# Gates and ups in seven products of quarters, for the last two token blocks of a two-layer fp32 kernel

## The reference

```python
h2 = rmsnorm(x, norm2_g[l])
gate = jnp.einsum('bsd,df->bsf', h2, w_gate[l])      # 1024 -> 2816
up = jnp.einsum('bsd,df->bsf', h2, w_up[l])          # 1024 -> 2816
x = x + jnp.einsum('bsf,fd->bsd', jax.nn.silu(gate) * up, w_down[l])
return rmsnorm(x, final_norm_g)
```

## Time and profile before

| | |
|---|---|
| median of 3 runs | 3772.93 us (3771.32 to 3776.09) |
| profiled execution, its own time | 3776.57 us |
| its span in the trace | 3774.2 us |
| busy: PE, PEld | 3707.6 us (98%), 3087.4 us (82%) |
| busy: DVE, ACT, POOL | 1829.6 us (48%), 1381.0 us (37%), 462.8 us (12%) |
| DMA | 799.34 MB, mean 212 GB/s |
| stage E and F of token block 2 | 2919 to 3342 us |
| stage E and F of token block 3 | 3342 to 3774 us |

### The profile page before, as it was taken

How to read it: one execution, slowest core, us unless ns; L and a number is a source line. 1 busy time by engine, 2 the same in 40 slices (tenths; PEclk the granted TensorE clock), 3 DMA queues, 4 the chain that set the end, 5 groups by cost and what they waited for, 6 DMA issues and landing times.

```text
span 3774.2 us, 58634 instructions
## 1 busy us (share of the span) xinstructions
PE 3707.6 (98%) x24136; PEld 3087.4 (82%) x24136; DVE 1829.6 (48%) x3365; ACT 1381.0 (37%) x2503; POOL 462.8 (12%) x237
## 2 busy tenths in 40 slices
PE   8999999999999999999999999999999999999999
PEld 6888788978897888976887779888777888887887
DVE  5657625451644455557655665554654222232223
ACT  4332421321232454565656655545552200020001
POOL 2001130000000000233233330000001000000000
PEclk9999999999999999999999999999999999999999
DMA  8756686557655877866666656545325655464554
GB/s 309 273 185 229 236 290 245 209 202 251 218 193 194 279 254 245 272 208 223 228 224 219 207 197 225 169 148 180 130 104 187 229 189 190 181 236 175 184 199 158
DMA packets 198874, 799.34 MB, mean 212 GB/s; under 512 B 20816, under 2 KB 70224, under 8 KB 130384
## 3 DMA queue, kind: packets, MB, share of 16 engines
q1 hardware_dynamic: 198608, 795.59, 60.7%
HBM read 594.18 MB, written 201.33 MB: 211 GB/s over the span
## 4 chain that ended last, share of the span: by engine, by line
PE 92%; DVE 4%; ACT 2%; issue 1%; DMA 1%; SPq 0%; DVEq 0%; ACTq 0%
PE bank L1402 87%; PE bank L1406 4%; DVE P L2484 1%; DVE P L2486 1%; DVE R L2145 0%; ACT P L1940 0%; ACT P L1939 0%; DVE Z1a L2192 0%; DVE Qb L2235 0%; SPq L2688 0%; DVE Tb L2236 0%; DMA slot<-Wd 0%; ACT L1939 0%; DMA KS<-Kd 0%; DVE Kb L2237 0%
## 5 line engine op out<-in xcount | busy, mean ns | idle before, releaser
L1402 PE MATMUL bank<-Z1a,slot 128*128 128x512 f32 x3048 | 786.1, 402 | 9.4 <-DVE slot L2083 9.4
L1402 PE MATMUL bank<-Z1b,slot 128*128 128x512 f32 x3048 | 780.9, 401 | 4.5 <-DVE Z1b L2192 4.4
L1402 PE MATMUL bank<-slot,Z0b 128*128 128x512 f32 (+1 forms) x3504 | 708.9, 353 | 7.2 <-DVE AF L2214 5.3
L1402 PEld LDWEIGHTS bank<-Z1a,slot 128*128 128x128 f32 x3048 | 568.0, 190 | 141.2 <-DVE slot L2083 9.4
L1402 PEld LDWEIGHTS bank<-Z1b,slot 128*128 128x128 f32 x3048 | 565.5, 189 | 139.1 <-issue 6.8
L1402 PEld LDWEIGHTS bank<-slot,Z0b 128*128 128x128 f32 x3504 | 563.0, 189 | 99.8 <-DVE AF L2214 6.0
L2648 POOL TENSOR_TENSOR slot<-raw,slot 128x1024 fp32r<-128x1024 f32 x110 | 289.9, 2643 | 645.5 <-ACT slot L1823 645.4
L2145 DVE SCALAR_TENSOR_TENSOR R<-bank,small,R 128x512 f32<-128x512 f32 x352 | 261.1, 749 | 208.2 <-PE bank L1402 207.7
L1402 PE MATMUL bank<-KS,DQ 128*128 128x512 f32 (+3 forms) x960 | 281.4, 389 | 9.3 <-DMA KS<-Kd 4.8
L2452 DVE TENSOR_SCALAR_CACHE_REDUCE P<-bank 128x512 f32<-128x512 f32 (+3 forms) x320 | 189.2, 608 | 199.0 <-PE bank L1402 198.4
L2660 POOL TENSOR_TENSOR Z0b<-AF,Z0b 128x512 fp32r<-128x512 f32 x88 | 126.6, 1439 | 1235.2 <-ACT Z0b L2013 1235.2
(11 more groups left out here) (235 smaller groups left out, 4551.2 us busy)
## 6 DMA issues: line engine op xcount, KB each, us to landing
slot<-Wd SPq DMA_DIRECT2D x390, 1024.0 KB, 4.9
Wd<-slot SPq DMA_DIRECT2D x130, 1024.0 KB, 6.8
raw<-in_wts_dram SPq DMA_DIRECT2D x130, 512.0 KB, 4.2
DQ<-Qd SPq DMA_DIRECT2D x192, 128.0 KB, 3.7
DV<-Vd SPq DMA_DIRECT2D x60, 256.0 KB, 4.5
KS<-Kd SPq DMA_DIRECT2D x24, 512.0 KB, 7.5
KS<-Kd SPq DMA_DIRECT2D x24, 384.0 KB, 6.9
zraw<-Yd SPq DMA_DIRECT2D x16, 512.0 KB, 5.5
```

The lines of the kernel that those rows point to most:

```text
L1402: return e.matmul(o, a, b, start=start, stop=stop, skip_group_check=True)
```

## The change

For token blocks 2 and 3 and slices 1 to 10, gate and up of a block b are taken as one product of 2 x 2 quarters: rows are gate and up, the 1024 input features are cut in two halves of 512, and the tokens in two halves of 256. Winograd's form of Strassen's algorithm needs seven products of quarters instead of eight; each is 4 x 3 matmuls of 256 columns. The order is 11, ST2, ST1, ST3, S4, T4, 12. Three banks are in use by one block (rotating over five that attention used before): 11 and then 12 add into the first, ST2, ST3 and T4 into the second, ST1 and S4 into the third, and what stands in a bank is read between two products.

- Four sums of weight quarters (S1 to S4) are made for each block: the two tiles are loaded once more as given (2 x 512 KB), GpSimd makes four adds of 128 x 512 (`sa`), ScalarE the large parts (`sh`), VectorE the small parts (`sl`).
- Four sums of feature quarters are made once per token block (`ta` on GpSimd, 128 x 1024 each, `th`, `tl`). For them, ScalarE writes each transposed feature group a second time, unsplit (`Bt`).
- ScalarE copies product 11 (`p1`); VectorE adds it or a former sum to each product (`cx`, 5 adds of 128 x 256), and the gate's factors are multiplied in two halves.
- Of the up's tile only the second half is loaded from `Wd`.
- Gates, ups and their two evictions at these blocks are gone: 2 x 24 matmuls of 512 columns.

```diff
+SEVEN = (2, 3)
+P_11, P_ST2, P_ST1, P_ST3, P_S4, P_T4, P_12 = range(7)
+SEVEN_BANKS = (2, 3, 4, 5, 6)
+SEVEN_ROLE = (0, 1, 2, 1, 2, 1, 0)
...
-            self.evac(label, ("act", 600), ("dve", 750))
+            self.evac(label, ("act", 1250 if s in SEVEN else 600), ("dve", 750))
...
+    def weight_sums(self, s):
...
+        for b in range(2, NF):
+            t = 0.0
+            if b > 2:
+                yield ("sa", s, b - 1)
+                t = P.end["sa", s, b - 1]
+            for x in range(2):
+                t = self.dma(("rf", s, b, x), 524288, t)
+            yield t
...
+            if b > 2:
+                yield ("sl", s, b - 1, 3)
+                yield P.end["sl", s, b - 1, 3]
+            t = P.put(("sa", s, b), ("pool", 5300), after=t)
+            if b > 3:
+                yield ("pr", s, b - 2, P_S4)
...
+        for i in (1, 0, 2, 3):
+            t = P.put(("sh", s, b, i), ("act", 610), after=t)
+            yield t
+            P.put(("sl", s, b, i), ("dve", 690), after=t)
...
+            P.put(("pr", s, b, i), ("pe", 12 * 117), after=t)
+            now = P.clock["pe"] + 180
+            if i == P_11:
+                P.put(("p1", s, b), ("act", 400), after=now)
+            elif i == P_12:
+                P.put(("ev", ("Fg", s, b)), ("dve", 850), ("act", 640), after=now)
+                P.put(("ev", ("Fu", s, b)), ("dve", 700))
+            else:
+                P.put(("cx", s, b, i), ("dve", 430), after=now)
...
+            def product(s, b, i):
...
+                elif i == P_ST3:
+                    pe.wait_ge(*dve_cx("cx", s, b, P_ST2))
+                elif i == P_S4:
+                    pe.wait_ge(*dve_cx("cx", s, b, P_ST1))
+                elif i == P_T4:
+                    pe.wait_ge(*dve_cx("cx", s, b, P_ST3))
+                else:
+                    pe.wait_ge(*act_p1("p1", s, b))
...
+                for k in range(4):
...
+                    mm(o, hi[:, tok(k)], bh, k == 0 and i in (P_11, P_ST2, P_ST1), False)
+                    mm(o, hi[:, tok(k)], bl, False, False)
+                    x = mm(o, lo[:, tok(k)], bh, False, k == 3)
...
+            def partial(s, b, i):
...
+                if i == P_ST2:
+                    to, x = pu[:, :], p1[:, :]
+                elif i == P_ST1:
+                    to, x = py[:, :], p1[:, :]
...
+                e.tensor_tensor(to, o, x, ALU.add).then_inc(*dve_cx.inc("cx", s, b, i))
...
+            def seven_gate(s, b):
+                g = GS[b % 2]
+                dve.wait_ge(*dve_cx("cx", s, b, P_S4))
+                e.tensor_tensor(g[:, 256:512], g[:, 256:512], factors[:, 256:512], ALU.mult)
+                dve.wait_ge(*pe_pr("pr", s, b, P_12))
+                e.tensor_tensor(g[:, 0:256], bank[seven_bank(s, b, P_12)][:, 0:256], factors[:, 0:256], ALU.mult).then_inc(
+                    *dve_g.inc("ev", ("Fg", s, b)))
...
+            def weight_sums(s, b):
+                g, u = (x[:, :].rearrange("p (a n) -> p a n", a=2) for x in raw)
+                for i in range(2):
+                    pool.wait_ge(*d_rf[i]("rf", s, b, i))
+                if b > 2:
+                    pool.wait_ge(*dve_sh("sl", s, b - 1, 3))
...
+                sums = ((u[:, 0, :], u[:, 1, :], ALU.add), (SF[:, 0, :], g[:, 0, :], ALU.subtract),
+                        (g[:, 0, :], u[:, 0, :], ALU.subtract), (g[:, 1, :], SF[:, 1, :], ALU.subtract))
...
+            def weights_as_given(s, b, x):
+
+                if b > 2:
+                    sp.wait_ge(*pool_sa("sa", s, b - 1, 3))
```

More of the change, by code:

```diff
@@ L183, in weight_order, with tile_blocks @@
     return order
+UPS = [T_F + 4 * sl + 2 * max(0, sl - 1) + 2 * k + 1 for sl in range(NF // 2) for k in range(2)]
+def tile_blocks(S):
+    order = weight_order(S)
+    n = len(order) - S * (N_TILES - T_E)
+    return [((i - n) // (N_TILES - T_E) if i >= n else -1, t) for i, t in enumerate(order)]
 def chunks(n):
@@ L214, in __init__ @@
         self.used = {}
+        self.pairs, self.pair_tiles = [], {}
+        self.halved = {i for i, (s, t) in enumerate(tile_blocks(S)) if s in SEVEN and t in UPS[2:]}
         self.G = {}
@@ L259, in fetch @@
             else:
-                P.end[("w", j)] = self.dma(("wf", j), 1048576, t)
+                P.end[("w", j)] = self.dma(("wf", j), 524288 if j in self.halved else 1048576, t)
     def left(self, j):
-        self.P.end["left", j] = self.P.end[("mm",) + self.used[j]]
+        self.P.end["left", j] = self.P.end[self.used[j]]
         self.fetch()
@@ L323, in mm @@
         for j in tiles:
-            self.used[j] = (label, part)
+            self.used[j] = ("mm", label, part)
     def evac(self, label, *steps):
@@ L767, in phase_e @@
             P.add(self.features2(s, cg), True)
+        if s in SEVEN:
+            P.add(self.token_sums(s), True)
+            P.add(self.weight_sums(s), True)
         P.add(self.norm2(s), True)
@@ L816, in phase_f @@
                     yield ("ev", ("Fu", s, 0))
+                if s in SEVEN and sl:
+                    yield from self.seven(s, b, t)
+                    P.add(self.split_act(s, b), True)
+                    t += 2
+                    continue
                 yield from self.fm(("Fg", s, b), t, 1, zr, ("dve", 690), ("act", 610), behind=() if b else (("ev", ("rb", s)),))
@@ L826, in phase_f, with seven @@
         P.put(("F done", s))
+    def seven(self, s, b, t):
+        P = self.P
+        jg, ju = yield from self.take(2, t)
+        self.pairs.append((s, b))
+        self.pair_tiles[s, b] = (jg, ju)
+        for i in range(7):
+            t = P.end["w", ju if i == P_T4 else jg]
+            if i in (P_ST1, P_ST2, P_ST3, P_S4):
+                k = ("sl", s, b, {P_ST1: 0, P_ST2: 1, P_ST3: 2, P_S4: 3}[i])
+                yield k
+                t = max(t, P.end[k])
+            if i in (P_ST1, P_ST2, P_ST3, P_T4):
+                k = ("tl", s, {P_ST1: 0, P_ST2: 1, P_ST3: 2, P_T4: 3}[i])
+                yield k
+                t = max(t, P.end[k])
+            yield t
+            P.put(("pr", s, b, i), ("pe", 12 * 117), after=t)
[7 more added lines that the diff above has]
+                P.put(("cx", s, b, i), ("dve", 430), after=now)
+            if i == P_T4:
+                self.used[ju] = ("pr", s, b, i)
+                self.left(ju)
+            yield None
+        self.used[jg] = ("pr", s, b, P_12)
+        self.left(jg)
     def split_act(self, s, b):
@@ L1190, in build @@
         pool_as = signal("pool_ff", of("as"))
+        pool_ta = signal("pool_token_sums", of("ta"))
+        pool_sa = signal("pool_weight_sums", [st + (i,) for st in of("sa") for i in range(4)])
         pool_cv = signal("pool_conv", of("cv halo"))
@@ L1198, in build @@
         d_z = landed("d_z", of("zf"))
+        d_rf = [landed(f"d_rf{i}", [st for st in of("rf") if st[3] == i]) for i in range(2)]
         d_R = [landed(f"d_R{c}", [st for st in order if st[0] in ("x0 in", "x1 in") and st[-1] == c]) for c in range(NT)]
@@ L1253, in weights_used @@
         def weights_used(j):
-            label, part = plan.used[j]
+            st = plan.used[j]
+            if st[0] == "pr":
+                return pe_pr(*st)
+            _, label, part = st
             return pe_g("ev", label) if final(part, label) else pe_half("half", label)
@@ L2117, in group_out @@
                 if by_act(label) and label not in gates:
+                    return
+                if ph in ("Fg", "Fu") and label[1:] in plan.pairs:
+                    (seven_gate if ph == "Fg" else seven_up)(s, label[2])
                     return
```

188 lines of the change are left out of this document (185 added, 3 removed).

## The result

| | before | after |
|---|---|---|
| median (range), four runs each on one chip | 3774.51 (3771.32 to 3777.41) | 3736.72 (3732.92 to 3738.93) |
| ratio (95% interval) | | 0.9899 (0.9882 to 0.9916) |
| span of the profiled execution | 3774.2 | 3731.2 |

The profiled execution after took 3732.92 us, the lowest of its four, and had the highest mean granted clock of them (0.996, the others 0.993 to 0.995). Between the spans lie 43.0 us, between the medians 37.8. The forecast was 46 by its own sum and a median of 3727.

A forecast was written before the change was run, and what follows sets the result against it. TensorE was taken to bound the kernel. Matmuls -56.0, waits in blocks +3, stage starts +4, first changed blocks +3 gave -46 us: 3776.6 to 3730.6, as a median 3727, range 3717 to 3755.

The forecast's parts named there:

- Matmuls: Gates and ups in 40 blocks: 11.20 us removed, 9.80 added per block, a gain of 56.0 us.
- no fixed cost to be seen: 256-column matmuls, read from the projection stage: 116.7 ns each, with no fixed cost on top.
- Rival 3: Seven products: shorter matmuls run slower than in the projection; at 133 ns the gain would be gone; chance 0.03.
- Waits inside a block: TensorE waiting for VectorE's reads between products: 0.08 us per block, 3 us in all, bounds 0 and 16.
- Turns: VectorE operations with two SBUF inputs and GpSimd operations wait for each other, up to 1.29 us per weight part.
- seven us: ScalarE's 0.42 us copy of product 11 was said to have seven us before it is needed.
- Supply: Weight sums for the next block, made while earlier blocks multiply: an 11.2 us cycle, hidden in 15.4, no cost.
- 4 us to spare: Margin claimed for making weight sums: a cycle of 11.2 us within the block's 15.4.
- Start of a stage: Second ScalarE pass over transposed features at two feed-forward starts: 2.1 us each, 4 in all, bounds 1 and 9.
- I assume it stays of that length: Slow clock after the wait at a feed-forward start: twelve matmuls take 4.42 us instead of 2.96, assumed unchanged.
- First changed blocks: First changed blocks of each feed-forward stage, waiting for their sums: 3 us in all, bounds 0 and 10.
- rival 1: Weight parts wait 1.29 us on GpSimd, delaying reads: 1.3 us per block, about 3776; full 0.05, partial (3740 to 3755) 0.22.

The follow-up runs named there:

- e_all32: Changed kernel with 32 unused bytes per partition ahead of everything, slots included, and 32 more ahead of the activations; span 3719.0 us.
- e_best2: e_align with SH moved on by another 32 bytes and the plain copy of the last two transposed features made last; median 3719.42 us, ratio 0.9852.
- e_slotw: Changed kernel with four products reading the gate's tile in its slot instead of the weight sums, which are still made; span 3730.2 us.
- e_read2: Changed kernel with VectorE's adds of products from PSUM to an SBUF partial each done twice; span 3742.7 us.
- F2: Not a run: the feed-forward stage of token block 2; 375.30 us in the kernel before, 353.14 in the changed one.
- F3: Not a run: the feed-forward stage of token block 3, with the tail; 383.6 us in the kernel before, 359.0 in the changed one.
- E2: Not a run: the projection stage ahead of the feed-forward stage of token block 2; 48.11 us in the kernel before, 1.66 more in the changed one.
- E3: Not a run: the projection stage between the feed-forward stages of token blocks 2 and 3; 47.89 us in the kernel before, 49.53 in the changed one.
- e_quiet: Changed kernel without sums, second weight loads or extra feature pass; the seven products read plain features and the gate's tile; span 3725.4 us.
- e_align: Changed kernel with 32 unused bytes per partition moving activations, token sums and weight sums onto a multiple of 64; span 3718.5 us.

## Right and wrong, step by step

1. **Matmuls, the mis-sized term.** "116.7 ns each" for the new products, from the earlier trace rows, was 120.0 for 48 and 118.3 for 36 of a block's 84. 0.43 us in each of 20 rounds is 8.6 us less gain. The count (84 for 48) and the 233.3 held. The form was taken from the right row, but "no fixed cost to be seen" was read from a place where the operands lay otherwise: slot as moving and Z as stationary operand, the reverse of the products. That the 120.0 comes from SH and the operand beside it having the same remainder, e_all32 and e_best2 show, and e_slotw fits. The rest, 118.3 against 116.7, is not explained; the projection of block 2, with 117.8 for 204 matmuls, was a sign in the kernel before that 116.7 can't be counted on. Rival 3 (slower than in the projection) is true by 3 ns, a sixth of the way to the 133 at which it would have decided.
2. **Waits inside a block, right, the cost too high.** Forecast 3 us (0 to 16), measured none in the steady rounds; e_read2 shows how near it was. Turns occur and are paid by idle engines. One reading was wrong and did no harm: the copy of product 11 has not "seven us", since the read of ST2 already adds it (`partial` takes `p1`). In the round shown it ends at 3135.93 and that read starts at 3136.99, so it has 1.06 us to spare.
3. **Supply, right.** Hidden in the steady state, with less room than "4 us to spare" says: 2.6 us more per block cost 16 us in F2 and F3, most of it in the first blocks; 5.2 more cost 100. What the estimate lacked is the chain of queues behind a late sum.
4. **Start of a stage, right.** Forecast 2 x 2.1 us, 4 in all; the projections E2 and E3 lost 1.65 each (1.1 of it the longer waits on Z1a shown above), the wait on Z1b 0.73 each: 4.8. The timeline shows the row of work that was foretold, with the plain copy (L1990) between the split passes:

```profile
2975.30 0.67 ACT L1990 ACTIVATE Bt<-bank,pvt 128x512 f32<-128x512 f32 x1
...
2975.87 0.68 ACT L1992 ACTIVATE Z1b<-bank,pvt 128x512 fp32r<-128x512 f32 x1
...
2976.58 0.75 DVE L2419 SCALAR_TENSOR_TENSOR Z1b<-bank,pvt,Z1b 128x512 fp32r<-128x512 f32 x1
...
2977.39 1.67 PE L1550 MATMUL bank<-Z1b,slot 128*128 128x512 f32 x6 [2.65 <-DVE Z1b L2419]
...
2979.34 3.35 PE L1550 MATMUL bank<-Z1a,slot 128*128 128x512 f32 x12
```

   "I assume it stays of that length" of the slow clock failed in our favour: the next 12 matmuls take 3.35 us, not the 4.42 of the earlier trace rows, though the wait before them is longer. The clock fell twice before and not after. From the end of the wait on Z1b to the third group of matmuls behind it the kernel before takes 6.77 us and the changed one 5.15, so it is worth 1.6 us each, 3.2 in the spans. In e_slotw it fell in F3 after the same wait of 2.65 us, in e_quiet in F2 after 1.92, so this part is luck and not a merit of the change.
5. **First changed blocks, right:** forecast 3, measured waits of 0.98 and 0.69 in the first two of block 2, which cost 2.5 from start to start, and nothing in block 3. But TensorE waited for reads of products that came late in VectorE's queue, not for weight parts. The chain was priced with GpSimd operations of 1.29 us; the first four weight sums took up to 2.27, 7.5 us in all instead of 5.2, as they ran beside parts with two SBUF inputs on VectorE:

```profile
2983.66 1.32 POOL L2944 TENSOR_TENSOR SF<-raw 128x512 f32<-128x512 f32 x1
2985.06 2.16 POOL L2944 TENSOR_TENSOR SF<-SF,raw 128x512 f32<-128x512 f32 x1
2987.18 2.27 POOL L2944 TENSOR_TENSOR SF<-raw 128x512 f32<-128x512 f32 x1
2989.41 1.75 POOL L2944 TENSOR_TENSOR SF<-raw,SF 128x512 f32<-128x512 f32 x1
```

   In the steady rounds all 48 of block 2 from 3030 us on took 1.28 to 1.31. So the turns of rival 1 cost something only where the stage starts.

The sum with the measured terms: -56.0 + 8.6 + 4.8 + 2.5 - 3.2 + 0.5 (ahead) = -42.8, measured -43.0. The medians lie 37.8 apart and not 43: the profiled execution after is the lowest of its four and has the highest granted clock, the one before (3776.57) is above its median. Without the luck of the clock the sum is -39.6, near those 37.8. Between this and the forecast of 46 the rate of the matmuls takes 8.6 us; all waits together, put at 10, came to 7.3.

## What to carry to other kernels

Price a matmul by a row in which both operands lie where the new ones will lie, moving and stationary in the same roles; the shape alone left 2 to 7 ns per matmul open, which is most of a percent in a kernel bound by TensorE. Before rewriting an algorithm, try shifting the operands by 32 bytes: here that alone gave 29.4 us, and it took a third off what the rewrite was worth. In a ring of in-order queues, slack counted on one engine is an upper bound, since a late step also holds what stands behind it on every other queue.

## What the runs showed that was not expected

- Rate of matmuls at the full granted clock, by the remainders of the operands' start addresses by 64 (moving, stationary). 512 columns: (0, 0) and (32, 32) 226.7 ns; (32, 0) and (0, 32) 233.3. 256 columns: (0, 0) and (32, 32) 120.0; (32, 0) 118.3; (0, 32) 116.7 with slot and Z0, but 118.3 with TS and SH. The same remainder is thus good for long and bad for short matmuls. What tells 116.7 from 118.3 stays open, and it is not the place alone: in E2, (0, 32) with slot and Z0 gave 117.8 first and 116.7 later. Other remainders were not tried.
- The Trainium skill (SBUF — State Buffer, "Who interferes with whom") has TensorE read its moving and its stationary operand through two independent ports. That rule gives no reason for a difference by the place of one relative to the other; e_all32 and e_align against the changed kernel show 6.6 ns of one.
- The same wait ahead of the same matmuls is followed by a granted clock of one half in some executions and not in others (2.65 us: not in the changed kernel, yes in F3 of e_slotw).
